# The turned keys of a chunked RWKV-7 scan by row-tiled transposes, and a new order of the engines' lists

## What is computed

```python
def update(s, w_t, k_t, v_t, kk_t, a_t):
    sa = jnp.einsum('ebhvk,ebhk->ebhv', s, kk_t)
    return s * w_t[..., None, :] - sa[..., :, None] * (kk_t * a_t)[..., None, :] + v_t[..., :, None] * k_t[..., None, :]
# forward over context then latents; the second direction over the flipped sequence
s, ys = lax.scan(step, s0, xs + (tm(r),))      # step: update, then ys = einsum('ebhvk,ebhk->ebhv', s, r_t)
```

## Time and profile before

| | us |
|---|---|
| median of 3 runs | 2462.98 (2462.48 to 2466.24) |
| profiled execution | 2464.82 |
| its span, first to last instruction | 2463.0 |
| TensorE busy | 2216.2 (90%) |
| six full rounds of the scan, 1597.6 to 1940.6 | 343.0 |

### The profile page before, as it was taken

One profiled execution on the slowest core, in us unless ns is written; L12 is line 12 of the kernel. 1 busy time (PEld: TensorE's weight loads), 2 busy tenths in 40 slices (PEclk: granted clock), 3 DMA queues, 4 the chain that ended last, 5 costly groups with the idle time before them and its releaser, 6 DMA issues. The chain is left out here.

```text
span 2463.0 us, 50823 instructions
## 1 busy us (share of the span) xinstructions
PE 2216.2 (90%) x22528; PEld 1842.0 (75%) x22528; DVE 942.2 (38%) x1500; ACT 688.3 (28%) x1059; POOL 852.2 (35%) x692
## 2 busy tenths in 40 slices
PE   5899989989699999999958998888888887999997
PEld 3788765555399999999926996777776665888785
DVE  3102265990320000022289214777777524000123
ACT  4110166421320000022232123555555223101112
POOL 2132300000233443434306445333333243666662
PEclk8999999999799999999979999999999988999998
DMA  6555530001012112111112444323233131222221
GB/s 247 214 192 215 194 135 18 1 8 69 26 52 68 60 60 68 60 60 60 45 37 77 118 131 116 65 56 59 56 63 62 23 117 55 94 94 94 85 99 64
DMA packets 175508, 210.32 MB, mean 85 GB/s; under 512 B 124791, under 2 KB 133751, under 8 KB 168152
## 3 DMA queue, kind: packets, MB, share of 16 engines
q1 hardware_dynamic: 175320, 207.49, 27.3%
HBM read 184.65 MB, written 22.81 MB: 84 GB/s over the span
## 5 line engine op out<-in xcount | busy, mean ns | idle before, releaser
L254 POOL CAST TMP_r<-WR 128x1024 fp32r<-128x1024 f32 x120 | 127.2, 1060 | 718.4 <-DMA WR<-in_ffn_w_dram 437.1
L273 PE MATMUL PS<-H_r,TMP_r 128*128 128x384 f32 (+1 forms) x1088 | 330.2, 359 | 11.6 <-DVE Y_r L490 11.6
L273 PE MATMUL PS<-Y_r,TMP_r 128*128 128x384 f32 (+1 forms) x1088 | 329.9, 358 | 3.7 <-DVE H_r L490 3.7
L256 POOL TENSOR_TENSOR WR_r<-WR,TMP_r 128x1024 fp32r<-128x1024 f32 x120 | 289.2, 2410 | 9.6
L413 DVE TENSOR_TENSOR P<-TMP,PS 128x768 f32 (+1 forms) x44 | 36.1, 821 | 562.5 <-PE PS L273 562.5
L273 PEld LDWEIGHTS PS<-H_r,TMP_r 128*128 128x128 f32 x1088 | 202.5, 190 | 28.3 <-DVE Y_r L490 12.6
L273 PEld LDWEIGHTS PS<-Y_r,TMP_r 128*128 128x128 f32 x1088 | 201.3, 189 | 19.3 <-DVE H_r L490 4.0
L273 PE MATMUL PS<-H_r,WR_r 128*128 128x384 f32 x736 | 191.6, 342 | 0.0
L396 ACT ACTIVATE TMP<-PS 128x768 f32<-128x768 f32 (+1 forms) x44 | 31.0, 705 | 526.1 <-PE PS L273 526.1
L590 PE MATMUL PS<-H_r,TMP_r 128*128 128x384 f32 x704 | 151.9, 338 | 3.2 <-DVE H_r L628 2.2
L273 PE MATMUL PS<-Y_r,WR_r 128*128 128x512 f32 x352 | 139.2, 396 | 0.0
(11 more groups left out here) (327 smaller groups left out, 4468.0 us busy)
## 6 DMA issues: line engine op xcount, KB each, us to landing
WR<-in_ffn_w_dram SPq DMA_DIRECT2D x88, 512.0 KB, 3.4
TMP<-in_mod_w_dram SPq DMA_DIRECT2D x40, 1024.0 KB, 4.8
WR<-in_down_dram SPq DMA_DIRECT2D x44, 512.0 KB, 3.4
WR<-in_mix_w_in_dram SPq DMA_DIRECT2D x24, 512.0 KB, 6.9
WR<-in_rw_w_rkv_dram SPq DMA_DIRECT2D x24, 512.0 KB, 4.2
P<-in_mod_w_dram SPq DMA_DIRECT2D x4, 2048.0 KB, 22.0
vkr_dram<-extra SPq DMA_DIRECT2D x16, 384.0 KB, 4.8
scan_front<-vkr_dram SPq DMA_DIRECT2D x16, 384.0 KB, 3.6
```

What stands on the lines that cost most here:

```text
L254: nc.gpsimd.tensor_copy(hi, raw).then_inc(weights_hi, 1)
L256: nc.gpsimd.tensor_tensor(lo, raw, hi.bitcast(F32), ALU.subtract).then_inc(weights_split, 1)
L273: last = nc.tensor.matmul(PS[:, bank + b, 0:h1 - h0], w, x[:, h0:h1], start=k + p == 0, stop=k == CT - 1 and p == 2)
```

## The change

`turned` uses transposes in place of matmuls against the identity. For the first head (partitions 0 to 63) one transpose takes 64 rows x 128 tokens, two chunks at once, and writes 128 partitions x 64 columns. For the second head the window of 128 tokens is moved on by one chunk, so that the chunk that must land on the upper partitions does so; its last chunk pair wraps round and is done by one 64-token transpose and one 64 x 64 matmul. That is eleven transposes of 64 x 128, one of 64 x 64, and one matmul (two instructions): 14 instructions. `solve` reads the second head's upper half one place earlier to match.

The rest of the change is a new order of the lists. The rounds begin at -2 in place of -3 (the first had nothing to do). In the tables below `0` is tile i, `1` tile n, `2` tile c, `-1` tile i - 1.

```diff
-            (0, "ta tx tb u1_0 u1_1"), (1, "l01 l11"), (0, "u2_0 u2_1 BV_1 u3_0 BV_0"), (-1, "var"), (0, "u3_1 oo_0"),
-            (1, "A_0"), (0, "oo_1"), (1, "A_1"), (0, "oo_2 mr_0"), (1, "kT_1"), (0, "mr_1 mr_2"), (-1, "vr"),
-            (0, "n_0 cg n_1 yt c0_1 c1_1"), (1, "tB_1"), (0, "c0_2 c1_2"), (1, "tK_0"), (0, "c0_3 c1_3"), (1, "kT_0"),
-            (0, "c0_4 c1_4"), (1, "tB_0"), (0, "c0_5 c1_5"), (1, "KD_0"), (0, "c0_6 c1_6"), (1, "KD_1"), (2, "kk"),
-            (0, "c0_7 c1_7"), (1, "tV"), (0, "c0_8 c1_8"), (1, "tK_1"), (0, "c0_9 c1_9"), (1, "CK_0"),
-            (0, "c0_10 c1_10"), (1, "CK_1"), (2, "kr"), (0, "ys"), (2, "l00 l10"), (0, "mean")))
+            (0, "ta tx tb"), (1, "l01 l11"), (0, "u1_0 u1_1 BV_0 u2_0 u2_1 BV_1"), (-1, "var"), (0, "u3_0 u3_1 oo_0"),
+            (1, "A_0"), (0, "oo_1"), (1, "A_1"), (0, "oo_2 mr_0 mr_1"), (1, "kT_1"), (0, "mr_2 n_0"), (-1, "vr"),
+            (1, "tB_1"), (0, "n_1 cg yt c0_1 c1_1"), (1, "tK_0"), (0, "c0_2 c1_2"), (1, "kT_0"), (0, "c0_3 c1_3"),
+            (1, "KD_0"), (0, "c0_4 c1_4"), (1, "tB_0"), (0, "c0_5 c1_5"), (1, "KD_1"), (2, "kk"), (0, "c0_6 c1_6"),
+            (1, "tV"), (0, "c0_7 c1_7"), (1, "tK_1"), (0, "c0_8 c1_8"), (1, "CK_0"), (0, "c0_9 c1_9"), (2, "kr"),
+            (0, "c0_10 c1_10"), (1, "CK_1"), (0, "ys"), (2, "l00 l10"), (0, "mean")))
         DV = Marks(dve_done, (
-            (1, "scan_0 scan_1"), (0, "u1_0 u1_1"), (1, "kin_1"), (0, "u2_0 u2_1"), (1, "kin_0 ba_0"), (0, "u3_0"),
-            (1, "bt_0 ba_1 bt_1"), (0, "u3_1"), (1, "kd_0 mA_0"), (-1, "rec"), (1, "mA_1 kd_1"), (0, "m_0 r_0"),
...
+            (0, "yx"), (1, "scan_0 scan_1 kin_0"), (0, "u1_0 u1_1"), (1, "ba_0"), (0, "u2_0"), (1, "ba_1 kin_1"),
+            (0, "u2_1 u3_0"), (1, "bt_0"), (0, "u3_1"), (1, "bt_1 mA_0 kd_0 mA_1"), (-1, "rec"),
+            (0, "m_0 r_0 m_1 r_1 m5_0 m5_1"), (1, "kt_0 kd_1"), (-1, "f1"), (0, "n_0"), (1, "acc_1 rt_1"), (-1, "f2"),
...
         PO = Marks(pool_done, (
-            (1, "s00 s10 sub turn off_0 off_1"),))
+            (0, "off_0"), (1, "s00 s10 sub turn off_1")))
@@ scan_sp, SyncE's list of a round
                     sp.wait_ge(dve_done, DV["mA_1", n])
                     gram_out(n, 1)
+                    if n:
+                        values_of(n)
                     blocks_back(n, 0)
                     blocks_back(n, 1)
...
-                            sp.wait_ge(dve_done, DV["accr", n])
+                            sp.wait_ge(dve_done, DV["rt_0", n])
                         keys_of(c)
                         queries_of(c)
+                    if c:
+                        lora_of(c)
                 if here(n):
                     sp.wait_ge(pool_done, PO["turn", n])
                     blocks_out(n, 0, XB, inv16_out)
-                    blocks_out(n, 2, YB, lower_out)
-                    turned_out(n)
                     if here(i):
                         sp.wait_ge(pe_done, PEM["yt", i])
                     sp.wait_ge(inv16_out, 16 * n + 16)
                     compact_back(n, 0, XC, x0_in)
+                    sp.dma_start(G2S, g2[n]).then_inc(gate2_in, 16)
+                    sp.dma_start(G2S2[0:GR, :], g2s[n]).then_inc(gate2_in, 16)
+                    blocks_out(n, 2, YB, lower_out)
+                    turned_out(n)
                     sp.wait_ge(lower_out, 32 * n + 32)
                     compact_back(n, 2, YC, y0_in)
...
-                if here(c):
-                    if c:
-                        values_of(c)
-                if here(c + 1):
-                    if c + 1:
-                        if here(c):
-                            sp.wait_ge(pe_done, PEM["l11", c])
-                        lora_of(c + 1)
@@ scan_pool, GpSimd's list of a round
                 if here(n):
+                    unit(n)
+                if here(i):
+                    others(i, 0)
+                if here(n):
                     pool.wait_ge(act_done, AC["t00", n])
                     gate(n, 0)
...
-                    unit(n)
                     substitute(n)
                     pool.wait_ge(pool_done, PO["sub", n])
                     turn(n)
-                    others(n, 0)
                     others(n, 1)
@@ scan_pe
             def turned(n, e):
                 name = f"kT_{e}"
                 b = front(name, n)
+                low, high = H2
                 for j in range(6):
-                    for h, q in HQ:
-                        t = slice(128 * j + 64 * q, 128 * j + 64 * q + 64)
-                        last = nc.tensor.matmul(PS[H2[q ^ h], b + h, 64 * j:64 * j + 64], KIN[e][H2[h], t], IDENT2[H2[h], :],
-                                                start=True, stop=True)
+                    at = slice(64 * j, 64 * j + 64)
+                    nc.tensor.transpose(PS[:, b, at], KIN[e][low, 128 * j:128 * j + 128], IDENT2[low, :])
+                    if j < 5:
+                        nc.tensor.transpose(PS[:, b + 1, at], KIN[e][high, 128 * j + 64:128 * j + 192], IDENT2[high, :])
+                    else:
+                        nc.tensor.transpose(PS[low, b + 1, at], KIN[e][high, 128 * j + 64:128 * j + 128], IDENT2[high, :])
+                        last = nc.tensor.matmul(PS[high, b + 1, at], KIN[e][high, 0:64], IDENT2[high, :], start=True, stop=True)
                 PEM.done(last, name, n)
@@ solve
                         kr = H2[q ^ h]
+                        at = (j - 1) % 6 if h > q else j
                         last = nc.tensor.matmul(PS[H2[q], b + h, 128 * k:128 * k + 128], UO[kr, e, h, j, :],
-                                                beside(KINT[kr, e, h, j, :], BVT[kr, e, h, j, :]),
+                                                beside(KINT[kr, e, h, at, :], BVT[kr, e, h, j, :]),
                                                 start=True, stop=True)
```

More of the change, by code:

```diff
@@ L1976, in __init__ @@
                 self.sem, self.made = eng_sem, 0
-                for it in range(-3, CT + 1):
+                for it in range(-2, CT + 1):
                     for ahead, names in order:
@@ L2034, in order @@
             return c + l if e == 0 else c[::-1] + l[::-1]
-        ROUNDS = [(it, it + 1, it + 2) for it in range(-3, CT + 1)]
+        ROUNDS = [(it, it + 1, it + 2) for it in range(-2, CT + 1)]
         def here(n):
@@ L2562, in scan_pe @@
                 if here(i):
-                    chain(i, 7)
+                    chain(i, 6)
                 if here(n):
@@ L2567, in scan_pe @@
                 if here(i):
-                    chain(i, 8)
+                    chain(i, 7)
                 if here(n):
@@ L2587, in scan_pe @@
                         yield
+                if here(i):
+                    chain(i, 10)
+                if here(n):
+                    gram_rest(n, 1)
                 if here(i):
@@ L2697, in scan_act @@
                 if here(n):
-                    falling(n, 0)
-                    rate(n, 1)
-                if here(i):
-                    act.wait_ge(pe_done, PEM["BV_0", i])
-                    values(i, 0)
+                    falling(n, 1)
                 if here(i - 1):
@@ L2732, in scan_act @@
                         yield
+                if here(i - 1):
+                    act.wait_ge(dve_done, DV["rec", i - 1])
+                    AC.done(nc.scalar.activation(FIN.rearrange("p (k t) -> p k t", t=TC),
+                                                 VROOT.unsqueeze(2).broadcast_to([128, 8, TC]), ACT.Copy), "vwide", i - 1)
+                if here(n):
                     act.wait_ge(pe_done, PEM["kT_1", n])
                     turned(n, 1)
-                    ends(n, 1)
+                    act.wait_ge(pe_done, PEM["tB_1", n])
+                    if here(i):
+                        act.wait_ge(pe_done, PEM["n_1", i])
+                    tokens(n, "tB_1", TOKB[:, 1])
                 if here(i):
@@ L2894, in scan_dve @@
             for i, n, c in ROUNDS:
+                if here(i):
+                    v.wait_ge(y0_in, 16 * i + 16)
+                    for b in range(4):
+                        last = nc.vector.tensor_scalar(XY[:, 2:4, :, :, BK * b:BK * b + BK].rearrange("p a h j t -> p (a h j) t"),
+                                                       YC, ROWB[:, b:b + 1], None, ALU.mult)
+                    DV.done(last, "yx", i)
                 if here(n):
@@ L2899, in scan_dve @@
                     sums(n, 1)
+                    v.wait_ge(act_done, AC["ep_0", n])
+                    keys(n, 0)
                 if here(i):
@@ L2906, in scan_dve @@
                 if here(n):
+                    v.wait_ge(act_done, AC["rate_0", n])
+                    based(n, 0)
+                if here(i):
+                    v.wait_ge(pe_done, PEM["u2_0", i])
+                    sweep(i, 2, 0)
+                if here(n):
+                    v.wait_ge(act_done, AC["rate_1", n])
+                    based(n, 1)
                     v.wait_ge(act_done, AC["ep_1", n])
@@ L2947, in scan_dve @@
```

(26 more changed lines are left out.)

174 lines of the change are left out of this document (70 added, 104 removed), and 18 rows, old and new, of tables (AC, DV).

## The result

The median is 2476.27 us (2471.31 to 2479.14 in four runs) against 2462.73 for the kernel before, timed beside it: a ratio of 1.0054, 95% interval 1.0037 to 1.0071. The change made the kernel slower by about 13 us. The forecast was 2461.9, and the time lies above the range of 2447 to 2474. The profiled execution took 2476.6 us.

The account below looks back on a forecast made before the run. TensorE bounds a round, with a loop through DRAM ending last in three of six. Terms +1.1 - 1.7 - 1.8 + 0 + 0.9 + 0.4 = -1.1 on 2464.8 give 2463.7; median 1.8 lower, 2461.9 us; range 2447 to 2474.

Parts of the forecast that it names:

- YC's way is longer: SyncE stores YB after XC's request and both g2 loads; YC some 2 us later, off_0 at 1766.8, both covered narrowly.
- values_of: SyncE issues this 384 KB load ahead of blocks_back: 0.3 us in three rounds, +0.9 us, between 0 and +8.
- Rival C: The way through DRAM becomes the bound, YC landing after cen: 1.6 us a round, +9.6; 2472 us, chance 0.16.
- The turned keys: On TensorE, a call with transposes takes 0.87 us, 0.07 more than now: +1.1 us in 16 calls.
- rival B: Transposes (calls at 0.40 to 0.6 us, -3 to -6) and fetches (-2.8) do more: 2456 us, chance 0.13.
- The serial end: The twelve weight loads of a turned-keys call on TensorE run one after another, 1.55 us a call: +12.0 us.
- Fewer instructions: 136 fewer TensorE instructions a round shorten its "issue" waits by 0.21 us a round: -1.7 us in eight rounds.
- tb to u1: On TensorE, l01 and l11 placed between these two cover the 0.3 us wait for ScalarE's copy: -1.8 us.
- yx and the stretch to the mask: VectorE's yx, 1.41 us, moves between ta and the second mask and fits: 0, or up to 1.4 us a round.
- The start: Before the first full round, where TensorE waits idle for ScalarE, off_0 comes last by 0.4 us: +0.4 us.
- Rival A: The new order closes half of the 3.5 us a round of waits for other engines, 10.5 us: 2452.5, chance 0.22.
- Rival D: Transposes bring TensorE one more half-rate clock stretch a round: +9 us, 2471 us, chance 0.09; sign PEclk 0.94 or less.

Follow-up runs that it names:

- e3: The changed kernel with off_0 ahead of unit on GpSimd: 2473.49 us, ratio 1.0034 to the kernel before.
- e4: The changed kernel with SyncE storing YB and its turned form right behind XB, g2 loads last: 2468.87 us, ratio 1.0025 to the kernel before.
- e5: The changed kernel with both off_0 ahead of unit on GpSimd and YB stored early on SyncE: 2473.24 us, ratio 1.0041 to the kernel before.
- e10: The changed kernel with values_of alone put back at the end of SyncE's round: 2472.78 us, ratio 1.0036 to the kernel before.
- e6: e5 with values_of also put back at the end of SyncE's round: 2462.6 us, ratio 1.0004 to the kernel before.
- e1: The kernel before with only the transposes for the turned keys, all lists in the old order: 2462.67 us, ratio 0.9992 to the kernel before.
- e2: The changed kernel with the old matmuls for the turned keys, so the new order alone: 2473.7 us, ratio 1.0048 to the kernel before.
- e12: e1 with four more VectorE multiplies of 128 x 512 a round, both inputs in SBUF: 2475.8 us.
- e13: e1 with four more VectorE multiplies of 128 x 512 a round, one input in PSUM: 2470.7 us.

## Why the prediction was wrong

**The step that failed** is "YC's way is longer ... some 2 us later in all" with off_0 at 1766.8, "0.8 us before ta. Both are covered, narrowly." Counted from the end of the turn, off_0 was to be ready after 9.7 us; it is after 11.1 to 12.2 (five rounds), so it holds ta in every round, by 1.0 to 1.9 us. YC was to be spread 2 us later than the 9.1 us before; it is 12.9, so 3.8. The order of events was read rightly. What was mis-sized is the issue of the first g2 load, which now stands right behind XC's request. The same load before and after, six rounds each (duration ns min/median/max):

```profile
L2166 SPq DMA_DIRECT2D scan_small<-in_rw_g_dram x6: 438/439/440, 1653.9 to 1940.0; - x6
```

```profile
L2164 SPq DMA_DIRECT2D scan_small<-in_rw_g_dram x6: 1654/1760/3226, 1649.4 to 1943.0; - x6
```

In the mean it takes 2.15 us in place of 0.44, and the 1.7 us between them come to nearly all of the 1.8 and 2.0 us by which YC and off_0 are later than counted. The row was on record: before, YC's request stood behind XC's, and the two took 2.75 us (YC's alone 1.05 to 2.19 in five of six rounds). The prediction left that long issue in YC's old way and gave the g2 load, which took its place, a short one. The landing was sized rightly: from the end of the last store's issue to unit are 1.6 to 3.4 us in five rounds, 2.3 in the mean (3.4 in the round shown).

This step is not the whole loss. Undone in part or whole, with all else as in the change, it leaves ratios of 1.0025 to 1.0041 where the change has 1.0054 (e3, e4, e5). The second term that failed is the 0.9 us for values_of: taken back alone it leaves 1.0036 (e10), and only in e6, with all three steps taken back, is the loss gone. How the loss divides between the two terms stays open, since the steps do not add up.

**Rival C** (2472, 0.16) was the right one: the way through DRAM becomes the bound. Its point of decision was YC more than 0.4 us later than counted; it came 1.8 us later. Both its signs are there, VectorE's wait for YC in front of the scans and ta's for off_0. Its price was 1.6 us a round, and the round grew by 2.3; that the wait of ta was not in the price is part of it.

**values_of** was put at 0.3 us in three rounds. It is 0.6 to 1.0 a round at its place over all six, within the bound of 1.27; what it cost in time, 2 to 11 us, reaches past the bound of 8.

**The turned keys** were put at +1.1 us (0.87 a call). The call shown takes 0.59, the others 0.52 as a rule: 8 x (0.80 - 0.55) and 8 x (0.70 - 0.55) are -3 us, inside rival B. The middle taken between the two ends was wrong because I held the load of 128 columns at 0.117 us whatever the rows, and the two halves at two side by side; the pairs come every 0.06. The serial end, +12.0 us, gives 2472.8, so the range took it in and did not leave it out, as the prediction says.

**Fewer instructions**: -0.21 us a round was forecast for the "issue" waits. It was 1.3 in e1 and 1.1 after, 30.4 to 24.0 us in all. It gave no time that e1's interval shows. The prediction's own first section had said that a shorter TensorE list gives nothing in three of six rounds, yet the sum counted this gain, and the next, in full.

**tb to u1**: the 1.8 us wait for ScalarE's copy is gone from the list of waits, as forecast, and gave nothing for the same reason.

**yx and the stretch to the mask**: counted as unchanged, it grew by 0.82 us a round. GpSimd's solve was not a term at all; it grew by 0.56, from VectorE's operations that read SBUF alone.

**The start** was +0.4: the first mean came 2.0 us earlier.

**Rival A** fell: waits for other engines rose from 20.8 to 30.8 us. **Rival D** named 0.94 or less as its sign, and the clock was at 0.94; yet it is not the cause. e1, with all the transposes, has 0.98, and e2, with none, 0.95. The lower level of 1.2 GHz stands behind TensorE's waits at the round's border. The two windows behind the mean of the round shown, columns as in the earlier trace rows:

```profile
1714.30:1717.30 3.00, 1.12 (x2) 0.30 (x3) 0.69 (x1) 2.24 (x3) 2.56 (x4) 0.98 0.65 67
1717.30:1720.30 3.00, 2.98 (x80) 3.00 (x82) 1.69 (x5) 1.37 (x2) 0.72 (x1) 0.50 0.27 26
```

TensorE was busy for 1.12 of the first three us, and in the next three the clock was 0.50. Behind the six means that follow the first, the second such window is at 0.64 or below in five of six rounds after, and in one of six before. So the clock adds to the loss behind the waits, as e5's row shows too; how the 9.9 us more of busy time divide between it and other causes was not measured. The sign should have been tied to the place of the transposes.

## What to carry to other kernels

Where two loops are nearly as long as each other, price what is "covered, narrowly" by the slowest row of its kind, and give the sum an expected cost, not nought: a cover of under 1 us against a way of three DMAs was no cover. Here the long issue went with the place in the queue and not with the transfer that stood there, so ask of a moved list on what it falls next. When one queue's order changes, follow every buffer that its stores read to the engine that overwrites it, and to what is queued behind that. And try the parts of an order alone: here, in the old lists, one part gained 0.1 to 0.2%, one did nothing, and one cost as much as the whole.

## What the runs showed of the hardware

- Transposes of 64 rows x 128 columns, alternating between the two row halves, start in pairs every 0.06 us, 0.03 each; the operation behind a call of 14 instructions starts 0.52 to 0.59 us after it began as a rule.
- TensorE's waits named "issue" fell with the number of instructions more than in proportion: 4.2% fewer gave 26% less (30.4 to 22.5 us in e1, one execution each).
- VectorE operations with both inputs in SBUF stop GpSimd for some 0.4 of their 0.70 us (e12); with an input in PSUM they do not (e13).
- The issue of a small DMA on SyncE's queue took 0.33 to 0.45 us as a rule, and far more right behind the request of XC: 1.65 to 3.23 for the g2 load in all six rounds after, which took 0.44 at its old place, and 1.05 to 2.19 for YC's in five of six rounds before. An estimate of a queue's time by the short rows is too low.
- Behind an idle time of 4.05 us TensorE's granted clock was 0.50, and the mean's matmul took 2.07 us in place of 1.13 (e5).
